# The projections of a gated linear attention: seven half-size products a pair of output tiles in place of eight

## What is computed

```python
def gla_mixer(h, w_in, w_a2, b_a, o_gain, w_out):
    proj = h @ w_in                       # q 512, k 512, v 1024, g 1024, a_lr 16 columns
    q, k, v, g, a_lr = jnp.split(proj, ...)
    log_a = log_sigmoid(a_lr @ w_a2 + b_a) / 16
    o = gla_chunked(qh * DK ** -0.5, kh, vh, ah)      # 4 heads, keys of 128, values of 256
    o = rms_norm(o, o_gain)
    return (o * silu(g)) @ w_out

def gla_chunked(q, k, v, log_a):          # chunks of 64 tokens
    cum = cumsum(log_a) within a chunk
    q_in, k_in = q * exp(cum), k * exp(-cum)
    o_intra = causal(q_in @ k_in.T) @ v
    k_dec, decay = k * exp(cum_last - cum), exp(cum_last)
    state[n+1] = state[n] * decay + k_dec.T @ v      # one step a chunk
    return o_intra + q_in @ state[n]
```

## Time and profile before

| | us |
|---|---|
| median of three timed runs | 2948.27 (2944.46 to 2949.16) |
| the profiled execution | 2943.7 |
| its span, first to last instruction | 2942.0 |
| mean granted TensorE clock, share of full | 0.986 |
| TensorE, DVE, ACT, POOL busy, share of the span | 96%, 59%, 36%, 46% |

### The profile page before, as it was taken

How to read it: one execution, slowest core, us unless ns; L and a number is a source line. 1 busy time by engine, 2 the same in 40 slices (tenths; PEclk the granted TensorE clock), 3 DMA queues, 4 the chain that set the end, 5 groups by cost and what they waited for, 6 DMA issues and landing times.

```text
span 2942.0 us, 39246 instructions
## 1 busy us (share of the span) xinstructions
PE 2811.1 (96%) x13278; PEld 2178.3 (74%) x13278; DVE 1729.2 (59%) x2188; ACT 1064.0 (36%) x1407; POOL 1352.4 (46%) x1652
## 2 busy tenths in 40 slices
PE   5999999998999999999999999999999999997997
PEld 3788888866878877787778888777666667774875
DVE  7679999988273612663564323263466666666454
ACT  5343444444120100000233232132466666665232
POOL 2344444557754533545723233577432222223775
PEclk9999999999999999999999999999999999998998
DMA  7521122155421132112331111333300000000423
GB/s 302 181 70 63 62 67 68 63 185 176 137 68 54 40 133 79 44 43 87 113 101 37 37 36 36 125 92 90 117 29 30 29 29 29 29 29 19 158 81 115
DMA packets 89451, 241.16 MB, mean 82 GB/s; under 512 B 6960, under 2 KB 20352, under 8 KB 88576
## 3 DMA queue, kind: packets, MB, share of 16 engines
q1 hardware_dynamic: 59648, 172.58, 18.7%
q10 hardware_dynamic: 29696, 67.16, 6.3%
HBM read 207.20 MB, written 32.51 MB: 81 GB/s over the span
## 4 chain that ended last, share of the span: by engine, by line
PE 78%; DVE 9%; POOL 5%; issue 3%; ACT 3%; DMA 2%; ACTq 0%; POOLq 0%; SPq 0%; DVEq 0%
PE ps L650 21%; PE ps L652 20%; PE ps L651 20%; POOL t_wl L550 4%; PE ps L1202 2%; PE ps L1239 1%; POOL t_wh L545 1%; DVE ps L2276 1%; PE ps L1023 1%; PE ps L1025 1%; PE ps L1024 1%; DVE t_total L2779 1%; PE ps L1095 1%; DVE t_tmp L2378 1%; DMA t_ctxr<-ctxT 1%
## 5 line engine op out<-in xcount | busy, mean ns | idle before, releaser
L650 PE MATMUL ps<-t_h_hi,t_wh 128*128 128x512 f32 x2432 | 989.1, 407 | 27.0 <-POOLq L553 11.5
L652 PE MATMUL ps<-t_h_hi,t_wl 128*128 128x512 f32 x2432 | 965.4, 397 | 0.0
L651 PE MATMUL ps<-t_h_lo,t_wh 128*128 128x512 f32 x2432 | 963.9, 396 | 0.0
L550 POOL TENSOR_TENSOR t_wl<-t_wst,t_wh 128x256 fp32r<-128x256 f32 (+2 forms) x1224 | 939.8, 798 | 24.5
L545 POOL CAST t_wh<-t_wst 128x1024 fp32r<-128x1024 f32 (+2 forms) x306 | 317.8, 1039 | 1356.8 <-PE ps L652 1245.5
L650 PEld LDWEIGHTS ps<-t_h_hi,t_wh 128*128 128x128 f32 x2432 | 459.0, 189 | 177.9 <-issue 43.6
L652 PEld LDWEIGHTS ps<-t_h_hi,t_wl 128*128 128x128 f32 x2432 | 458.7, 189 | 111.2
L651 PEld LDWEIGHTS ps<-t_h_lo,t_wh 128*128 128x128 f32 x2432 | 459.7, 189 | 109.9 <-issue 6.1
L2276 DVE SCALAR_TENSOR_TENSOR ps<-t_upad,t_vec,ps 128x1024 f32<-128x1024 f32 x224 | 275.5, 1284 | 7.1 <-DVE ps L2270 0.9
L650 PE MATMUL ps<-t_y_hi,t_wh 128*128 128x512 f32 x512 | 206.1, 402 | 9.8 <-POOLq L553 7.9
L652 PE MATMUL ps<-t_y_hi,t_wl 128*128 128x512 f32 x512 | 202.6, 396 | 0.0
(11 more groups left out here) (353 smaller groups left out, 3906.0 us busy)
## 6 DMA issues: line engine op xcount, KB each, us to landing
t_wst<-w_even_in SPq DMA_DIRECT2D x40, 512.0 KB, 3.5
t_wst<-w_ple SPq DMA_DIRECT2D x64, 320.0 KB, 2.9
t_wst<-w_even_out SPq DMA_DIRECT2D x32, 512.0 KB, 3.6
t_wst<-w_fox_in SPq DMA_DIRECT2D x32, 512.0 KB, 3.6
t_modw<-w_mod SPq DMA_DIRECT2D x6, 2048.0 KB, 16.1
t_xr<-x_d ACTq DMA_DIRECT2D x6, 2048.0 KB, 13.2
t_wst<-w_gla_in SPq DMA_DIRECT2D x24, 512.0 KB, 3.8
t_wst<-w_odd_in_a SPq DMA_DIRECT2D x16, 512.0 KB, 3.5
```

Source lines behind the costliest of these rows:

```text
L550: pool.tensor_tensor(wl[b][:, c], wst[b][:, c], wh[b][:, c].bitcast(F32), ALU.subtract).then_inc(S("w_low"), 1)
L650: pe.matmul(o, w1, x1, start=start and k == 0, stop=False)
L651: pe.matmul(o, w1, x2, start=False, stop=False)
L652: last = pe.matmul(o, w2, x1, start=False, stop=stop and k == kts - 1)
```

## The change

Each pair of output tiles (128 features each) by 1024 features of input and 1024 tokens is treated as a 2 x 2 by 2 x 2 block product, with blocks of a tile by 512 input features by 512 tokens, and made by seven block products in place of eight (Strassen's scheme in Winograd's form). A block product is 4 x 3 = 12 matmuls of 512 columns, so a pair takes 84 in place of 96. There are ten such pairs: the gate pair of head 0, and Q/K, V and gates of heads 1 to 3. Head 0's Q, K and V stay as they were, but V's last part comes after its key transposes and scores.

On the activations' side four sums of blocks (t1 to t4) are made once, by POOL (`whole_h`), DVE and ACT, in the space where the gated outputs lay; those now go to memory (`store_gated`) and are reloaded at the end (`load_gated`). For each pair SP loads four raw blocks into `wst` (`load_pair`), a block when POOL has split what was there; DVE makes four sums of blocks (`sums`); POOL splits seven operands of 512 columns (`split_operand`) into a ring of four; TensorE makes the seven products in the order a11, a12, s2, s1, s3, s4, a22 (`pair`), two or three of them into one bank. Between products that share a bank ACT copies the bank's sum so far (`copied`), and DVE adds such copies to banks to get three of the four output quarters (`evacuated`); ACT takes the fourth (`plain`).

V comes out features by tokens now, so 16 transposes a head turn it before the chunks (`turn_gla_values`). The decay's small product stands inside the Q/K pair, after its first product, and uses the banks that held the outputs of the head before. In the last head the gate pair comes before the chunks; after them its outputs are scaled, gated and split by halves of the tokens, while TensorE makes the first two output tiles, as far as their operands are there. The loops over heads are written out, and semaphores that earlier phases are done with are used again (`AGAIN`). The core of the diff:

```diff
-    ("w_gla_in", 4, [1024] * 6),
+    ("w_gla_in", 1, [1024] * 4),
...
+GLA_PAIRS = ["G0"] + [kind + str(i) for i in range(1, 4) for kind in ("QK", "V", "G")]
...
+        return bank(6 + t if name in ("fout", "gout") and t < 2 else t % 4)
...
+    OPERANDS = ["a11", "a12", "s2", "s1", "s3", "s4", "a22"]
+    SOURCE = {"a11": raw_block(0), "a12": raw_block(1), "s2": s2[:, :], "s1": s1[:, :], "s3": raw_block(2),
+              "s4": s4[:, :], "a22": raw_block(3)}
+    SUMMED = {"s1": 1, "s3": 2, "s2": 3, "s4": 4}
+    def moving(name):
+        if name[0] == "t":
+            n = int(name[1])
+            return [(t_r[T_HI[n]][:, k * HALF:(k + 1) * HALF], t_r[T_LO[n]][:, k * HALF:(k + 1) * HALF])
+                    for k in range(4)]
+        k0, c = {"b11": (0, 0), "b21": (4, 0), "b22": (4, 1)}[name]
+        return [(hcol(h_hi, c, k0 + k), hcol(h_lo, c, k0 + k)) for k in range(4)]
+    MOVING = ["b11", "b21", "t2", "t1", "t3", "b22", "t4"]
...
+        def load_pair(n):
+            kind, row = GLA_PAIRS[n][:-1], int(GLA_PAIRS[n][-1]) * P
+            for r in range(4):
+                if n == 0:
+                    sp.wait_ge(S("w_split"), first["w_gla_in"] + 4 + 2)
+                else:
+                    sp.wait_ge(S("s_ready"), again("s_ready", 7 * (n - 1) + (1, 2, 5, 7)[r]))
+                    sp.wait_ge(S("s_sum"), again("s_sum", 4 * n))
+                if kind == "V":
+                    at = 2048 + r % 2 * 1024
+                    src = dram["w_gla_in"][row:row + P, at:at + 1024].rearrange("p (k v m) -> p k v m", k=4, v=2)
+                    sp.dma_start(raw_block(r).rearrange("p (k m) -> p k m", k=4), src[:, :, r // 2, :])\
+                        .then_inc(S(f"s_raw{r}"), 16)
+                else:
+                    at = (4096 if kind == "G" else 0) + r * HALF
+                    sp.dma_start(raw_block(r), dram["w_gla_in"][row:row + P, at:at + HALF]).then_inc(S(f"s_raw{r}"), 16)
...
+        def load_gated():
+            sp.wait_ge(S("s_used"), again("s_used", 7 * NPAIR))
+            sp.wait_ge(S("yg_stored"), again("yg_stored", 16 * 6))
+            for k in range(6):
+                sp.dma_start(col(y_lo, k).bitcast(F32), tile(y_d, k)).then_inc(S("yg_loaded"), 16)
...
+        def split_operand(n):
+            pair_, q = divmod(n, 7)
+            name = OPERANDS[q]
+            src = SOURCE[name]
+            if name in SUMMED:
+                pool.wait_ge(S("s_sum"), again("s_sum", 4 * pair_ + SUMMED[name]))
+            else:
+                raw_ = {"a11": "s_raw0", "a12": "s_raw1", "a22": "s_raw3"}[name]
+                pool.wait_ge(S(raw_), again(raw_, 16 * (pair_ + 1)))
+            if n < 4:
+                pool.wait_ge(S("w_used"), first["w_gla_in"] + 2 + 4)
+            else:
+                pool.wait_ge(S("s_used"), again("s_used", n - 3))
+            hi, lo = ring(wh, n), ring(wl, n)
+            pool.tensor_copy(hi, src).then_inc(S("s_high"), 1)
+            pool.wait_ge(S("s_high"), again("s_high", n + 1))
+            for z in range(2):
+                c = slice(z * 256, (z + 1) * 256)
+                pool.tensor_tensor(lo[:, c], src[:, c], hi[:, c].bitcast(F32), ALU.subtract).then_inc(S("s_low"), 1)
+            pool.wait_ge(S("s_low"), again("s_low", 2 * (n + 1)))
+            pool.sem_inc(S("s_ready"), 1)
...
+            if name == "w_gla_in":
+                split_tile(name, 0, 0, T, widths, 0)
+                split_tile(name, 0, 1, T, widths, 0)
+                split_tile(name, 0, 2, T, widths, 0)
+                pool.wait_ge(S("h_ready"), h_base("oout_b", 2))
+                whole_h(0, 0, t_f[0], 0)
+                split_tile(name, 0, 3, T, widths, 0)
+                whole_h(1, 0, t_f[1], 4)
+                for n in range(NPAIR):
+                    if n in (0, 3, 6):
+                        causal(n // 3)
+                    split_pair(n)
+                causal(3)
...
+        def pair(n, y, x, v, free=None, inside={}):
+            into = {"a11": y, "a12": x, "s2": y, "s1": v, "s3": y, "s4": v, "a22": y}
+            opens, closes = ("a11", "a12", "s1"), ("a12", "s4", "a22")
+            for q, name in enumerate(OPERANDS):
+                if q == 0 and free:
+                    free()
+                pe.wait_ge(S("s_ready"), again("s_ready", 7 * n + q + 1))
+                if name == "s2":
+                    if n == 0:
+                        pe.wait_ge(S("t_low"), again("t_low", 1))
+                    pe.wait_ge(S("s_copied"), again("s_copied", 3 * n + 1))
+                if name == "s1" and n == 0:
+                    pe.wait_ge(S("t_low"), again("t_low", 2))
+                if name == "s3":
+                    if n == 0:
+                        pe.wait_ge(S("t_low"), again("t_low", 3))
+                    pe.wait_ge(S("s_copied"), again("s_copied", 3 * n + 2))
+                if name == "s4":
+                    pe.wait_ge(S("s_copied"), again("s_copied", 3 * n + 3))
+                if name == "a22":
+                    if n == 0:
+                        pe.wait_ge(S("t_low"), again("t_low", 4))
+                    pe.wait_ge(S("s_out"), again("s_out", 3 * n + 2))
+                o = bank(into[name])
+                for k, (x1, x2) in enumerate(moving(MOVING[q])):
+                    c = slice(k * P, (k + 1) * P)
+                    w1, w2 = ring(wh, 7 * n + q)[:, c], ring(wl, 7 * n + q)[:, c]
+                    pe.matmul(o, w1, x1, start=(k == 0 and name in opens), stop=False, skip_group_check=True)
+                    pe.matmul(o, w1, x2, start=False, stop=False, skip_group_check=True)
+                    last = pe.matmul(o, w2, x1, start=False, stop=(k == 3 and name in closes), skip_group_check=True)
+                last.then_inc(S("s_used"), 1)
+                if q in inside:
+                    inside[q]()
...
+        gla_gates(0)
+        half_added("oout_b", 15)
+        take("w_gla_in", 0, 1)
+        project(wbuf("w_gla_in", 1), slot(1), h_hi, h_lo).then_inc(S("w_used"), 1)
+        pe.wait_ge(S("g_ab"), 1)
+        gla_values(0).then_inc(S("w_used"), 2)
+        gla_chunks(0)
+        gla_gate_pair(0)
+        for i in range(1, 4):
+            qk, vv, gg = 3 * i - 2, 3 * i - 1, 3 * i
+            pair(qk, 7, 5, 6, lambda: pe.wait_ge(S("g_rs"), i),
+                 {0: lambda: gla_gates(i), 2: lambda: pe.wait_ge(S("s_out"), again("s_out", 3 * (gg - 3) + 3))})
+            pair(vv, 4, 3, 2, lambda: pe.wait_ge(S("s_plain"), again("s_plain", gg - 2)))
+            if i == 3:
+                pair(gg, 7, 1, 0)
+                pe.wait_ge(S("s_out"), again("s_out", 3 * gg + 3))
+            pe.wait_ge(S("s_out"), again("s_out", 3 * vv + 3))
+            gla_turn_keys(i)
+            gla_scores(i)
+            turn_gla_values(i)
+            gla_chunks(i)
+            if i < 3:
+                gla_gate_pair(i)
...
+        pe.wait_ge(S("g_st"), 16 * 3 + 16)
+        gla_square_sum(3, 0, 4)
+        early_gout(0, range(6))
+        gla_square_sum(3, 1, 5)
+        pe.wait_ge(S("s_used"), again("s_used", 7 * NPAIR))
         end(pe)
-
+        early_gout(1, range(6))
+        early_gout(0, (6, 7))
+        early_gout(1, (6, 7))
...
+        for i in range(1, 4):
+            qk, vv, gg = 3 * i - 2, 3 * i - 1, 3 * i
+            copied(qk, 7, 6, 0)
+            gla_decay(i)
+            copied(qk, 7, 6, 1)
+            copied(qk, 7, 6, 2)
+            gla_growth(i)
+            store_gated(i - 1)
+            gla_shrink(i)
+            plain(qk, 7, kdt[:, 0:HALF])
+            copied(vv, 4, 2, 0)
+            gla_to_end(i)
+            copied(vv, 4, 2, 1)
+            copied(vv, 4, 2, 2)
+            plain(vv, 4, st[:, T:T + HALF])
+            if i == 3:
+                copied(gg, 7, 0, 0)
+                copied(gg, 7, 0, 1)
+                copied(gg, 7, 0, 2)
+                plain(gg, 7, silu_g[1][0][:, :])
+            keys_out(i)
+            for n in range(3):
+                values_out(i, n)
+            if i < 3:
+                out_squares(i)
+                gate_pair(i)
+        act.wait_ge(S("s_out"), again("s_out", 3 * NPAIR))
+        act.wait_ge(S("s_plain"), again("s_plain", NPAIR))
+        for c in range(2):
+            for v in range(2):
+                line.go(A(silu_g[v][c][:, :], silu_g[v][c][:, :], ACT.Silu))
+        line.sync()
+        act.sem_inc(S("g_g0"), 1)
+        act.wait_ge(S("yg_loaded"), again("yg_loaded", 16 * 6))
+        gated_high(0)
+        half_squares(0)
+        gated_high(1)
+        half_squares(1)
+        out_half_factor(0)
+        out_half_factor(1)
...
+        mask_and_copy(0)
+        wu(4)
+        sums(0)
+        states(0)
+        whole_low(0, 2)
+        whole_low(1, 1)
+        squares_added(0)
+        evacuated(0, 0, 5, att[:, 0:HALF])
+        whole_low(2, 3)
+        whole_low(3, 4)
+        evacuated(0, 1, 4, kdt[:, HALF:T])
+        outs_scaled(0)
+        evacuated(0, 2, 6, att[:, HALF:T])
+        sums(1)
+        for i in range(1, 4):
```

(89 more changed lines are left out.)

361 lines of the change are left out of this document (268 added, 93 removed).

## The result

The changed kernel takes 2950.05 us (median of 22 runs, 2944.61 to 2956.61), the kernel before 2945.28 (22 runs, 2940.68 to 2949.64). The ratio is 1.0015, with a 95% interval of 1.0010 to 1.0021: some 4.4 us slower. The forecast was no measurable change at 2946.5.

A forecast was written before the change was run, and what follows sets the result against it. TensorE, busy 96% of the span, was taken as the bound. Savings of 26.5 us against stalls and clock loss summed to +3.0 us on the profiled 2943.7, so 2946.7; called 2946.5, no measurable change, range 2940 to 2954 (2930 to 2960 with rivals).

The forecast's parts named there:

- (a): Head 0: TensorE stalls 3.2 us for the first state, behind DVE's sums and score mask.
- (b): Q/K pairs, heads 1 to 3: the product s3 waits for ACT's copy, behind DVE's late minimum; 7.8 us.
- (c): V pairs: late POOL operands, then a reload and DVE's sums delay V's last quarter; 7.8 us (0 to 11).
- (d): After the last head's chunks: late gated outputs delay the reload of x, so output tile 4 waits 7.5 us.
- (e): TensorE's clock falls to 1.2 GHz after two of the stalls, costing 3.2 us (0 to 11).
- removed from TensorE: Gated-attention stage: fewer Q/K, gate and V matmuls and the hidden wait on turned keys save 26.5 us.
- A: Q/K and V pairs: operand splits keep ahead as DVE and POOL interleave better; 2932.5 us, chance 0.33.
- B: Q/K and V pairs: the port shared with DVE makes POOL the bound; 2956 us, chance 0.22.
- C: Chunks of three heads: transposes and scores standing together lower the clock, 2 us each; 2952 us, chance 0.05.

The follow-up runs named there:

- the second profile: The changed kernel run once more with no edit, for another profile; it took 2944.42 us, its stage 397.3 us.

## Why the prediction was wrong

Each wait costs its idle time and some 0.17 more, because a matmul of 0.40 starts 0.23 after the one before it when nothing is waited for. With that, the sum as predicted and as the profile after has it:

| term | predicted | measured |
|---|---|---|
| (a) head 0, first state | 3.2 | 3.2 |
| (b) Q/K pair, three times | 7.8 | 5.3 |
| (c) V pair | 7.8 | 6.3 |
| (d) the end | 7.5 | 5.3 |
| (e) clock | 3.2 | 7.8 |
| fourth weight tile of head 0 (L1188) | none | 1.2 |
| sum of these | 29.5 | 29.1 |
| removed from TensorE | 26.5 | 25.9 (what 29.1 leaves of +3.2) |

**The step that failed** is the last one, from the sum to the forecast, and ahead of it term (e).

The sum of +3.0 says slower. I turned it into "no change" by setting it beside three runs with a median of 2948.3, while its rows come from one profiled execution of 2943.7. Over 22 runs the kernel before has 2945.28; the sum laid on that gives 2948.3, slower by 0.1%, where 2950.05 was measured.

For the clock (e) I took two drops of 1.6 and wrote that stalls ahead of small products lose less. In head 0 the reverse holds: after the gap of 3.03 the chunk products ran at 1.2 GHz and lost 6.1 in this profile, 1.5 to 6.1 in six, where output tiles 2 and 3 lost 1.7 after the gap of 3.86. The gaps before the key transposes lost 1.5 to 1.65 in 7 heads of 10, none of them in this profile.

That the sum of +3.0 lies so near the +3.2 of the stage is luck: (b), (c) and (d) were 6.2 too high together, (e) and the weight tile of head 0, which I had at nothing, 5.8 too low.

A typical execution probably loses more than the first profile. No profile of the changed kernel shows one at its median. The nearest are those of the two runs whose edits gave nothing, the minimum earlier and the end of the last head: 2948.25 and 2948.64, stages of 402.3 and 401.4, and the clock down behind both gaps of V.

**(a)** was right to 0.1: mask over at 1551.55 (1551.8 predicted), the four sums at 1555.43 (1555.5). But what the sums wait for on DVE is TensorE's last V product, which the prediction does not name:

```profile
1551.46 0.69 DVE L3013 TENSOR_TENSOR t_piece<-t_wst 128x512 f32<-128x512 f32 x1 [1.41 <-PE ps L1190]
```

**(b)** The mechanism was right, the size not: minimum, decay and copy ended 1.0 earlier than worked out. DVE's four sums and two products were done at 6.6 instead of 7.1, and the decay took 6.47 instead of 6.76. But what stood right behind, POOL, I priced in (c) alone.

**(c)** I had POOL's last V operand ready at 41.2 (its terms, 3.2, 29.4 and 9, add up to 41.6); it was 40.2 (1636.86, from 1596.7). The twelve operands paid 8.6 to DVE over an undisturbed 28.2, against the 9 charged. The Trainium skill, SBUF — State Buffer, section SBUF: two separate sides, has the port pair that DVE and POOL share locked for a whole instruction. By that rule I had put some 11 on POOL; the trace lies nearer to the charge from rows. DVE's own products lengthened beside POOL too (1.63 and 1.75 against 1.23), so the total does not show how long the pair was held. The gap of 3.0 before the key transposes was 2.2, at the place and with the releaser predicted.

**(d)** Size near, place wrong. I had tile 4 wait for the reload of x. In this profile DVE's first add to x ends at 1883.2 and TensorE passes on to tile 4 without a wait; in the second profile that wait is 0.9. What waits is tile 2: its split reuses the buffer of tile 0, which is held until the last gated outputs of its half arrive.

```profile
1867.66 1.10 POOL L634 CAST t_wh<-t_wst 128x1024 fp32r<-128x1024 f32 x1 [2.93 <-PE ps L817]
1868.84 3.73 POOL L639 TENSOR_TENSOR t_wl<-t_wst,t_wh 128x256 fp32r<-128x256 f32 x4
```

I did not follow the ring of two weight buffers into the output phase. How the 5 us there divide between this ring, the banks that tile 2 shares with the last outputs, and x close behind, stays open.

**The rivals.** A did not come: it has (c) and the clock at 0, and they took 6.3 and 7.8. B's condition is met, 3.07 an operand against the 2.80 from which it decides, but the stall of (b) hid it; it showed when that stall was removed. C, a clock that falls on transposes and scores by themselves, is excluded: in head 3, where no gap stands before them, the same 24 transposes and the scores ran at full speed in every profile, and in heads 1 and 2 wherever the gap was 1.3 or less. The Trainium skill, TensorE: Matmul & The Clock Gate, section Part 4: PE-mode transpose, says that transposes do not count as busy for the clock in the same way; 4.9 us of transposes and scores together, with no gap ahead, did not show it here. Whether transposes behind a gap make a fall likelier than other matmuls would, no run separates.

## What to carry to other kernels

Taking an eighth of the products from a bound engine paid here only once the queues that now prepare more operands were put in order: look for an operation that the bound engine needs soon and that stands behind one needed later, above all behind one that waits for a reload, and move it ahead. Four such moves turned 0.15% slower into 0.6% faster. When a removed wait gives nothing, look at the next releaser; a helper engine that was slower per operand than the bound engine needed only an earlier start here, since after its twelve operands it had nothing to do for a while (10.8 us in head 1). Price a gap of TensorE with what its clock loses behind it, and set a sum against the same execution that its rows come from, or against many runs, not a few.

## What the runs showed that I had not expected

A single gap of 3.0 us cost 1.5 to 6.1 us more by the clock than its length, in the same place of six profiles. Gaps of 1.6 before 512-column products never lowered the clock (18 of 18), gaps of 2.0 to 2.6 before 128-column transposes mostly did (7 of 10), and so did gaps of 1.9 to 2.4 before 512-column matmuls elsewhere (19 of the 30 counted above). So a wait a few tenths longer can cost nearly its own length again, and one profile of a kernel may show none of that loss.
